# Column sums behind the gate products, two output units ahead of the gate rows, and 18 homes for the experts' pieces

## What is computed

```python
def trunk_layer(x, mods, p, ctx_k, ctx_v):
    shift1, scale1, gate1, shift2, scale2, gate2 = mods
    h = modulate(rms_norm(x, p['g_pre_mix']), shift1, scale1)
    m, k, v = parallel_mixer(h, p, ctx_k, ctx_v)
    x = x + gate1 * rms_norm(m, p['g_post_mix'])
    h = modulate(rms_norm(x, p['g_pre_ffn']), shift2, scale2)
    f = expert_choice_ffn(h, p)
    x = x + gate2 * rms_norm(f, p['g_post_ffn'])
    return x, k, v
```

## Time and profile before

| | us |
|---|---|
| median of 3 runs | 2357.07 |
| profiled execution | 2359.29 |
| its span, first to last instruction | 2357.5 |
| TensorE busy (matmul) | 2209.2 |
| VectorE busy | 1086.6 |
| ScalarE busy | 319.1 |
| GpSimd busy | 122.3 |

### The profile page before, as it was taken

How to read it: one execution, slowest core, us unless ns; L and a number is a source line. 1 busy time by engine, 2 the same in 40 slices (tenths; PEclk the granted TensorE clock), 3 DMA queues, 4 the chain that set the end, 5 groups by cost and what they waited for, 6 DMA issues and landing times.

```text
span 2357.5 us, 26790 instructions
## 1 busy us (share of the span) xinstructions
PE 2209.2 (94%) x10616; PEld 1383.2 (59%) x10616; DVE 1086.6 (46%) x1770; ACT 319.1 (14%) x757; POOL 122.3 (5%) x130
## 2 busy tenths in 40 slices
PE   6999999999989999999999989999998888889886
PEld 3489964544779999999977753333332222222223
DVE  5188997647678778676663441110101010102114
ACT  3011110000223332001000021011110000000002
POOL 0011100000111121000000000100000000000000
PEclk9999999999999999999999999999999999999999
DMA  9965563443534354545452379999999999999997
GB/s 385 379 240 190 196 223 117 147 147 116 179 108 155 131 179 143 179 143 190 165 201 101 114 284 376 408 421 421 421 421 421 421 423 421 422 421 421 421 413 284
DMA packets 210292, 645.47 MB, mean 274 GB/s; under 512 B 10502, under 2 KB 80648, under 8 KB 161928
## 3 DMA queue, kind: packets, MB, share of 16 engines
q1 hardware_dynamic: 206248, 637.67, 70.0%
q10 hardware_dynamic: 3936, 6.27, 0.7%
HBM read 640.24 MB, written 3.67 MB: 273 GB/s over the span
## 4 chain that ended last, share of the span: by engine, by line
PE 74%; DMA 17%; DVE 4%; DVEq 2%; issue 1%; SPq 1%; ACT 1%; ACTq 0%; POOL 0%
PE PS L849 26%; DMA ring<-in_w_up 15%; PE PS L720 11%; PE PS L1457 9%; PE PS L1418 8%; PE PS L1256 4%; PE PS L1241 2%; PE PS L709 2%; PE PS L1382 1%; DMA ring<-in_w_down 1%; DMA ring<-in_w_ada 1%; PE PS L1495 1%; DVE RG L2986 1%; PE PS L1036 1%; PE PS L1360 1%
## 5 line engine op out<-in xcount | busy, mean ns | idle before, releaser
L1418 PE MATMUL PS<-ring,RF 128*48 128x512 f32 x1568 | 363.2, 597 | 62.1 <-DMA ring<-in_w_up 60.4
L2184 DVE SCALAR_TENSOR_TENSOR RG<-ring,SM,RG 128x512 f32<-128x512 f32 x450 | 330.6, 773 | 15.9 <-issue 0.6
L1418 PEld LDWEIGHTS PS<-ring,RF 128*48 128x48 f32 x1568 | 108.6, 123 | 300.0 <-issue 300.0
L720 PE MATMUL PS<-ring,RB 128*128 128x512 f32 x576 | 251.8, 593 | 0.0
L849 PE MATMUL PS<-RB,ring 128*128 128x192 f32 x1376 | 233.5, 327 | 0.2
L849 PEld LDWEIGHTS PS<-RB,ring 128*128 128x128 f32 x1376 | 226.1, 191 | 5.3 <-ACT RE L1661 0.8
L2981 DVE TENSOR_TENSOR RC<-RC,PS 128x512 f32<-128x512 f32 x84 | 56.4, 685 | 363.7 <-PE PS L1382 363.4
L1457 PE MATMUL PS<-ring,RF 128*48 128x512 f32 x864 | 194.7, 609 | 2.9 <-DVE RF L2990 2.9
L720 PEld LDWEIGHTS PS<-ring,RB 128*128 128x128 f32 x576 | 108.3, 190 | 127.6 <-issue 127.2
L2986 DVE TENSOR_TENSOR RG<-RF,PS 48x512 f32<-48x512 f32 x32 | 22.1, 690 | 307.3 <-ACT RF L1903 272.8
L1457 PEld LDWEIGHTS PS<-ring,RF 128*48 128x48 f32 x864 | 58.9, 126 | 133.6 <-issue 132.4
(11 more groups left out here) (414 smaller groups left out, 2639.9 us busy)
## 6 DMA issues: line engine op xcount, KB each, us to landing
ring<-in_w_down SPq DMA_DIRECT2D x124, 1024.0 KB, 14.2
ring<-in_w_gate SPq DMA_DIRECT2D x118, 1024.0 KB, 13.0
ring<-in_w_up SPq DMA_DIRECT2D x118, 1024.0 KB, 14.5
ring<-in_w_ada SPq DMA_DIRECT2D x48, 2048.0 KB, 9.1
ring<-in_w_in SPq DMA_DIRECT2D x38, 2048.0 KB, 8.9
ring<-in_w_attn_o SPq DMA_DIRECT2D x8, 2048.0 KB, 8.5
ring<-in_w_out SPq DMA_DIRECT2D x8, 2048.0 KB, 8.6
ring<-in_w_hy_o SPq DMA_DIRECT2D x4, 2048.0 KB, 9.8
```

The costliest lines, as they stand in the source:

```text
L720: last = mm(bank(b0 + m), lhs[:, h * HK + k, m * P:(m + 1) * P], ring[:, (n + h) % 4, k, :], start=(h == 0 and k == 0), stop=(h == 1 and k ...
L1418: last = mm(bank(n, p0=64 * u, p1=64 * u + SLOTS), xeT[:, 0, kk, :] if first else x_cur[:, kk, :], homes[home_of(at, 2 * i + u)][:, k * FF ...
L2184: last = stt(out=acc[c], in0=w, scalar=cond[:, kk, c:c + 1], in1=acc[c], op0=ALU.mult, op1=ALU.add)
```

## The change

It has three parts. In heads 4, 8 and 12 `ada_sums` moves behind the four gate units, `read_block` behind `proj_weights`, and STEPS gives head 3 four steps instead of six and head 15 six instead of four. For q = 0, two output units move ahead of the broadcast, and VectorE's `add_out(0, 11)` ahead of the gate rows. The pieces get 18 homes: RB takes the first extra homes and the experts' sum `facc`, RC the transposed rows `rT` (where mixT lay), `selG`, `sel_cur` and `ye`; XX is a new home; the router's tables move to RG and XX. Pieces are ordered by when homes come free, and piece 0 is issued after the fourth half block of w_out.

```diff
-        homes = [pieces[:, j, :] for j in range(8)] + [view(RC, j * 2 * FF, 2 * FF) for j in range(3)] + \
-            [view(RE, j, 2 * FF) for j in (8192, 10240, 6144)] + [view(RB, j * 2 * FF, 2 * FF) for j in range(3)]
+        homes = [pieces[:, j, :] for j in range(8)] + [view(RB, j * 2 * FF, 2 * FF) for j in (0, 2, 1)] + \
+            [view(RE, j, 2 * FF) for j in (10240, 8192, 6144)] + [view(RC, j * 2 * FF, 2 * FF) for j in range(3)] + \
+            [view(XX, 0, 2 * FF)]
...
-        selG, sel_cur = view(RB, 0, MT, NE // 2, P), view(RB, 3072, MT, P)
-        ye = view(RB, 4096, 4, NC_)
+        facc = view(RB, 0, MT, D)
...
-        facc = view(RC, 0, MT, D)
+        rT = view(RC, 0, KT, T)
+        selG, sel_cur = view(RC, 0, MT, NE // 2, P), view(RC, 3072, MT, P)
+        ye = view(RC, 4096, 4, NC_)
...
-        wr_amp = view(RE, 6144, 2, KT, 32)
-        wr_shift = view(RE, 7168, 2, KT, NE)
-        wr_sum, b_row = view(RE, 7680, 2 * NE), view(RE, 7712, 2, NE)
+        wr_amp = view(RG, 1024, 2, KT, 32)
+        wr_shift = view(XX, 3072, 2, KT, NE)
+        wr_sum, b_row = view(XX, 3584, 2 * NE), view(XX, 3616, 2, NE)
...
-        RING, SUMS, ROWS, SELS, OUTS = [0, 1, 2, 3, 4, 5, 6, 7], [8, 9, 10], [11, 12, 13], [14, 15], [16]
-        HOMES = RING + SUMS + ROWS + SELS + OUTS + RING + SUMS + ROWS + SELS + RING + ROWS + RING + ROWS + RING + ROWS[:1] + RING
+        RING_A, RING_B, RING = [0, 1, 2, 3], [4, 5, 6, 7], [0, 1, 2, 3, 4, 5, 6, 7]
+        SUMS, LATENT, CONTEXT, AHEAD, SELS, OUTS, FORMS = [8, 9, 10], [11], [12], [13], [14, 15], [16], [17]
+        HOMES = AHEAD + RING_A + SUMS[:1] + FORMS + SUMS[1:] + LATENT + RING_B + CONTEXT + SELS + OUTS + \
+            AHEAD + RING_A + SUMS + LATENT + RING_B + CONTEXT + SELS + \
+            FORMS + AHEAD + RING_A + LATENT + RING_B + CONTEXT + \
+            FORMS + AHEAD + RING_A + LATENT + CONTEXT + FORMS + AHEAD + RING + RING
...
             def first_expert():
-                for q in range(PIECES):
-                    if q < 8:
-                        slot_free(N_EX + q // 2)
-                    elif q == 11:
+                for q in range(1, PIECES):
+                    home = home_of(0, q)
+                    if q >= 18:
+                        piece_free(*behind(0, q))
+                    elif home < 8:
+                        slot_free(N_EX + home // 2)
+                    elif home in (8, 17):
+                        sp.wait_ge(unit, unit_at("out", 3, 3))
+                    elif home == 9:
+                        sp.wait_ge(unit, unit_at("out", 3, 4))
+                    elif home == 10:
+                        sp.wait_ge(unit, unit_at("out", 3, 6))
+                    elif home == 11:
+                        sp.wait_ge(wo_mul, 15)
+                    elif home == 12:
                         sp.wait_ge(wo_mul, 16)
-                    elif q == 13:
-                        sp.wait_ge(lg_sub, 1)
-                    elif q == 14:
+                    else:
                         sp.wait_ge(lg_mm, MT)
-                    elif q >= 17:
-                        piece_free(*behind(0, q))
-                    load_piece(0, q, home_of(0, q))
...
+            for c in range(4):
+                for h in range(2):
+                    half_block(N_WO + 2 * c + h, w_out, h, c)
+                if c == 1:
+                    sp.wait_ge(blocks_used, by_pe(N_WO - 2))
+                    load_piece(0, 0, home_of(0, 0))
...
                     attend(t - 1)
-                    if t % 4 == 0:
-                        ada_sums(15 + t // 4, to=MODS_AT)
                 scores(t)
...
                     gate_units(p, 0, 4)
+                    if t % 4 == 0:
+                        ada_sums(15 + t // 4, to=MODS_AT)
...
                 context_half(q, 1)
+                if q == 0:
+                    out_units(0, 0, 2)
                 if q < 2:
                     broadcast_gates(4 * q, 6, ones, diag_ready, g_bc, g_used)
...
-                out_units(q, 0, 4)
+                out_units(q, 0 if q else 2, 4)
...
-            pool.wait_ge(piece_used, 15)
+            pool.wait_ge(piece_used, 16)
...
-            STEPS = (2, 4, 4, 6) + (4,) * 12
+            STEPS = (2,) + (4,) * 14 + (6,)
...
                 maxima(t)
-                if t > 0 and t % 4 == 0:
-                    read_block(15 + t // 4)
                 normalise(t)
...
                     proj_weights(p)
+                    if t > 0 and t % 4 == 0:
+                        read_block(15 + t // 4)
...
                 third_out(q)
+                if q == 0:
+                    add_out(q, 11)
                 gate_rows(0, g_rows, 6, diag_ready, g_bc, g_used, 4 * q, 4 * q + 2)
                 gated_out(q, 0)
-                add_out(q, 11)
+                if q > 0:
+                    add_out(q, 11)
```

More of the change, by code:

```diff
@@ L381, in sem_of, with piece_sem, before_pieces @@
         def sem_of(home):
-            return home if home < 8 else min(8 + (home - 8) // 2, 11)
+            return home if home < 8 else (8, 9, 10, 13, 12, 11, 14, 15, 15, 14)[home - 8]
+        def piece_sem(home):
+            n = sem_of(home)
+            return piece_in[n] if n < 12 else landed[n - 12]
+        def before_pieces(home):
+            n = sem_of(home)
+            return 0 if n < 12 else arrived(N_EX + n - 16)
         def loads_of(e, q):
@@ L548, in _ @@
                 half_block(N_GA + 3 * p + 2, w_ada, p % 2, 20 + p // 2)
-            for c in range(4):
-                for h in range(2):
-                    half_block(N_WO + 2 * c + h, w_out, h, c)
             def gate_piece(w, e, i):
@@ L597, in early_expert @@
                     piece_free(*behind(e, q))
+                    if e == 1 and home_of(e, q) == 15:
+                        sp.wait_ge(piece_sem(16), before_pieces(16) + 32)
                     load_piece(e, q, home_of(e, q))
@@ L1228, in tile_logits @@
                     last = mm(bank(2, P, m * P, p0=32 * g, p1=32 * g + 32), wr_amp[:, min(m, 1), k, :],
-                              hT[:, k, m * P:(m + 1) * P], start=k < 4, stop=k >= KT - 4)
+                              rT[:, k, m * P:(m + 1) * P], start=k < 4, stop=k >= KT - 4)
                 last.then_inc(lg_mm, 1)
@@ L1395, in landing @@
                 def landing(q):
-                    pe.wait_ge(piece_in[sem_of(home_of(at, q))], (e - at) * 48 + 16 * loads_of(at, q))
+                    home = home_of(at, q)
+                    pe.wait_ge(piece_sem(home), (e - at) * 48 + (16 * loads_of(at, q) + before_pieces(home)))
                 if not first:
@@ L1482, in landing @@
                 def landing(q):
-                    pe.wait_ge(piece_in[q % 8], (e - 3) * 48 + 16 * (loads_of(3, 0) + q // 8))
+                    pe.wait_ge(piece_in[q % 8], (e - 3) * 48 + 16 * (loads_of(3, q % 8) + q // 8))
                 def gate_up(d, beside):
@@ L2880, in _ @@
                 dve.wait_ge(tr2, 8 + c + 1)
-                V.tensor_copy(hT[:, 4 * c:4 * c + 4, 0:P], bank(B_T[c]).rearrange("p (k t) -> p k t", k=4))\
+                V.tensor_copy(rT[:, 4 * c:4 * c + 4, 0:P], bank(B_T[c]).rearrange("p (k t) -> p k t", k=4))\
                     .then_inc(tr2_v, 1)
```

9 lines of the change are left out of this document (6 added, 3 removed).

## The result

| | before | after |
|---|---|---|
| median | 2357.88 us (6 runs, 2356.82 to 2360.15) | 2367.72 us (6 runs, 2363.53 to 2369.60) |
| profiled execution | 2359.29 | 2367.21 |
| its span | 2357.5 | 2365.4 |
| mean granted clock of TensorE | 0.988 | 0.984 |

The changed kernel is 9.8 us slower by the medians; the ratio, taken of the means, is 1.0038 (9.0 us) with a 95% interval of 1.0026 to 1.0050.

The account below looks back on a forecast made before the run. TensorE was taken to bound the kernel to about 1549 us, the transfer of the remaining expert pieces after. Terms +2.7 + 5.0 + 2.35 + 1.7 - 3.6 + 0.6 = +8.8 gave 2365.9 us, range 2355 to 2371.

Parts of the forecast that it names:

- the joint at piece 72: Expert loads: TensorE sets the time until about 1549 us, when it frees piece 72's place; transfers set it after.
- From this point on the end is fixed: After piece 72's issue at 1549.26, 312 pieces at 2.49 us and a tail remain; earlier loads can't move it.
- rival A: Expert loads: landed transfers, not TensorE's use of piece 64, decide; end up to 10.6 us earlier, 2346.5; chance 0.07.
- The homes: Expert pieces: 18 homes instead of 17 cost +0.6 us, bounds -2.5 and +1, as piece 72 waits for TensorE.
- the late link: New home list: piece 53's context home is freed some 9 us after piece 52's, holding all later pieces behind it.
- Head 4: TensorE stands 8.2 us instead of 5.5 before the column sums, the loss to the clock alike: +2.7 us.
- Heads 8 and 12: TensorE waits 2.5 us in each before the column sums, where it had no wait: +5.0 us together.
- I take one loss of 1.7 over the two heads, bounds 0 and 3.6: Heads 8 and 12: lower granted clock after the 2.5 us waits costs 1.7 us in all.
- The end of the heads: Two steps moved from head 3 to 15 take 2.9 us on VectorE, less slack, and reach a gate product: +2.35.
- Output products: Before the q = 0 broadcast: idle 1.5 us instead of 3.2, -1.8 standing and -1.8 clock, -3.6 us.
- The late w_hy_o: Heads 4 and 8: VectorE waits some 4 us for this load; TensorE needs the result a head later; priced at nothing.
- Rival D: VectorE's 4 us wait for w_hy_o reaches TensorE a head later, 1 to 2 us each, clock falls; 2372; chance 0.12.

Follow-up runs that it names:

- e3_homes: Kernel before with only the 18 homes and their order; 2358.74 us, ratio 1.0003 to the kernel before.
- e9_gap: Changed kernel, heads 4, 8, 12: last two steps between maxima and normalisation, fold right behind normalisation, sums behind probabilities; STEPS (2,) + (4,) * 12 + (6, 4, 4); 2346.31 us.
- e10_gap_oldhomes: Same edit of the changed kernel as e9_gap, but with the old 17 homes in the old order; 2345.84 us, ratio 0.9948 to the kernel before.
- e8_onestep: Changed kernel with STEPS (3,) + (4,) * 14 + (5,), one late step instead of two; 2361.11 us, ratio 1.0012 to the kernel before.
- e6_spread: Changed kernel with STEPS (2,) + (4,) * 13 + (6, 4), the two extra steps in head 14 instead of 15; 2366.33 us, ratio 1.0033 to the kernel before.
- e2_out: Kernel before with only the output products' part (two units of q = 0 ahead of the broadcast, add_out earlier); 2353.92 us, ratio 0.9986.
- e1_heads: Kernel before with only the heads' part (sums behind gate products, new STEPS, read_block late); 2370.85 us, ratio 1.0053.
- e7_behindproj: Changed kernel with the sums moved behind the probabilities, next queries and three projection products of the same head; 2368.64 us, ratio 1.0042 to the kernel before.
- e5_oldsteps: Changed kernel with the old STEPS, (2, 4, 4, 6) + (4,) * 12, sums still behind the gate products; 2350.69 us, ratio 0.9970 to the kernel before.

## Why the prediction was right

**What bounds the kernel: that TensorE's pace reaches the end is shown, the joint at piece 72 is not.** In the twelve kernels piece 72 stands -13.4 to +12.75 us from where the kernel before has it, and the end with it, to within 1 us, always with a gap of 8.8 to 9.3 us in SyncE's queue ahead of it. But every edit of TensorE's work acts before 1300 us, so a joint anywhere behind that would have moved alike; for the same reason the forecast didn't suffer from it. "From this point on the end is fixed" is a step of the prediction that the transfers of the kernel before contradict. Here are pieces 71 and 72, with their us from issue to landing (72 is issued at 1549.26), and a piece issued at 1366.47, 24 us after the last landing:

```profile
1539.65 0.33 SPq L579 DMA_DIRECT2D ring<-in_w_down  x1
ring<-in_w_down SPq DMA_DIRECT2D x1, 1024.0 KB, 15.4
...
ring<-in_w_gate SPq DMA_DIRECT2D x1, 1024.0 KB, 8.2
...
ring<-in_w_gate SPq DMA_DIRECT2D x1, 1024.0 KB, 4.8
```

Piece 71 lands at 1555.0, not at 1552.4 as walked, and 72 at 1557.5, just one transfer behind it, where on an empty queue it could have landed at 1554.1. So 72 waits for the transfers ahead of it, with 3.4 us to spare. In all twelve kernels it lands 2.4 to 2.6 us behind 71. From 1489 us on the pieces of the kernel before land 2.5 us apart up to 72, but for one at 3.6. The transfers are the bound well before 1549, and whether 2 or 3 us of TensorE between 1500 and 1549 would reach the end at all was not run. The condition of rival A, an old queue more than one piece behind at 1549, is met (2.3 pieces); its gain did not come.

**The homes: the size is right, the reason only in part.** +0.6 predicted, +0.1 in the trace to piece 72 (e3_homes), and the medians of e9_gap and e10_gap_oldhomes are 0.5 us apart, within their scatter. The reason given first, that 72 waits for TensorE, isn't it. Pieces 52 and 53 of e3_homes, issue and us to landing:

```profile
1494.12 0.33 SPq L590 DMA_DIRECT2D RE<-in_w_gate  x1
RE<-in_w_gate SPq DMA_DIRECT2D x1, 1024.0 KB, 10.5
1502.71 0.33 SPq L590 DMA_DIRECT2D RE<-in_w_up  x1
RE<-in_w_up SPq DMA_DIRECT2D x1, 1024.0 KB, 6.7
```

Piece 52 lands at 1504.6, 2.0 us earlier than in the kernel before (1506.6): up to there the new list does bring the transfers forward. Piece 53, the late link that the prediction named, is issued 8.6 us behind it and lands at 1509.4, against 1509.1 before, and the lead is gone. Whether a list without that link would gain wasn't run. The Trainium skill ("Perfetto Trace Analysis", "Optimization Strategy") takes a gap that repeats on the engine that should be saturated for a possible sign of too few buffers; in e3_homes one home more changed the time by nothing that can be measured. Nor did the 13 us by which TensorE was early in e9_gap make the homes worth anything.

**Head 4: the size was off.** Predicted was a wait of 8.2 for 5.5 and "the loss to the clock alike", +2.7. Measured: 7.60, and head 4 costs 1.1 us. The wait is 2.1 us longer rather than 2.7. The loss to the clock is 2.8 us where it was 3.1: from the sums to `attend` 8.83 us pass (701.48 to 710.31), where the same work at full speed takes 0.85 for the sums and 5.22 from the transposes to `attend` (777.86 to 783.08 in head 8 of the kernel before), 6.07. The kernel before needs 5.73 for that last part in head 4 (704.96 to 710.69), with its clock up: some 0.5 us of idle ahead of `attend`, for which the profile names no releaser, was in its head 4 and is gone here. The sum had no term for it.

**Heads 8 and 12: the standing was right, the clock too small.** 2.5 us of standing each, measured 2.38. But "I take one loss of 1.7 over the two heads, bounds 0 and 3.6" is the step that failed. Between `attend(7)` and `attend(8)` the changed kernel loses 5.84 us (763.72 and 783.08 before, 762.98 and 788.18 after), 3.5 of them beyond the standing, and 1.9 in head 12: 5.3 us of clock in all, outside the bounds. I had set the row with 3.24 us of idle against that with 1.56 and shared the difference; a wait of 2.38 us cost more than the 1.8 us of that longer one. e8_onestep and e9_gap show that it goes with the wait: 0.89 us, or none, and heads 8 and 12 run at full speed.

**The end of the heads: right in size (2.35; 2.2), off in place.** TensorE stands at two points, 0.76 and 1.49 us, where it had one of 0.45. That two steps put into head 15 are the cause, and could be had for nothing elsewhere, is only half shown: moved to head 14 they cost 0.4 us less (e6_spread), moved to head 13, with the fold early, they cost nothing (e9_gap).

**Output products: right.** -3.6, measured -3.63 between w_out and the broadcast of q = 1 here, and -3.62 in e2_out. That half of it is clock holds where the old wait brings the clock down; behind the heads' part it doesn't (e1_heads), and there, as in the changed kernel, the edit is worth half.

**The late w_hy_o: priced at nothing, and it cost nothing, for the reason given only in part.** VectorE waits 3.61 us for it in head 4, as foretold, and TensorE none in head 5. The slack was taken for that of the next head. e7_behindproj shows that it was the wait for the fold itself: take that away and TensorE stands 3.84, 3.27 and 3.43 us in heads 5, 9 and 13. Rival D was no rival in this kernel but is the next bound behind it.

**The sum.** Predicted +2.7 + 5.0 + 2.35 + 1.7 - 3.6 + 0.6 = +8.8. Measured in the trace +1.1 (head 4), +4.8 (standing of heads 8 and 12), +5.3 (their clock, less 0.4 that the trace wins back in head 5), +2.2, -3.6, +0.2: +9.6, and +9.8 in the medians. That the sum is within 1 us is partly luck: an error of -1.6 in head 4 and one of +3.6 in the clock came out, with the small terms, as one of 0.8. The rest of the 1.8 us is the base: the prediction started from a median before of 2357.07, and with six runs it is 2357.88.

## What to carry to other kernels

Before you move a consumer away from a late producer, look whether the producer moves too: in head 4, counted from its `attend`, TensorE came to the sums 12 us later and the fold was done 14 us later, and all that stood behind the sums (probabilities, queries) was made to wait. A wait is also a cover: each time one was taken away the next one behind it came up (the weights in e5_oldsteps, the w_hy_o load in e7_behindproj), so walk the whole head through without the wait before you count on it. And look for the place where the producer's engine is idle anyway: with the same two steps in the gap of 1.67 us or more in which VectorE waits for the exponentials, the fold right behind the normalisation and the sums behind the probabilities, a loss of 9.8 us became a gain of 11.7.

## What the runs showed of the hardware

The clock's price isn't a function of the length of the wait alone. In the kernel before 3.24 us of idle cost 1.8 us afterwards, in e1_heads the same 3.24 us cost nothing; 2.45 us in head 4 of e5_oldsteps cost nothing either (the 16 products behind it took 2.84 us), but 2.38 us in the changed kernel cost 3.5 in head 8 and 1.9 in head 12, and so again in e1_heads (5.88 and 4.25 us for the two heads with their standing). In e7_behindproj waits of 2.94, 3.27, 3.43 and 3.84 us were followed by 1.7, 1.7, 3.4 and 1.7 us of clock, by the granted clock of the stretches behind them (0.74 from 703.4 to 710, 0.73 from 795.6 to 802, 0.57 from 872 to 880, 0.74 from 718.4 to 725). Waits of 0.89 to 1.68 us cost no clock wherever I looked, and a stretch of the head phase without waits (e9_gap) was at full clock throughout. For a sum this means: a wait of 2.4 to 3.3 us may cost nothing or one and a half times its length again, and the bounds must say so. What decides between the two is not shown here.

A piece of 1.049 MB that finds the queue empty lands 4.8 us after its issue; in a full queue the pieces land 2.5 us apart, whatever their issue (8.2 and 15.4 us for pieces 72 and 71). So the time at which SyncE issues a load doesn't say what holds it: compare its landing with that of the load ahead of it.
